# Turned ring of the experts' weights: slots 3 and 4 fetched ahead, one copy of the normed rows, and a token list for the gathers

## The reference

```
def hier_moe(h, rg_w, rg_b, re_w, re_b, w_gate, w_up, w_down):
    gp = softmax(h @ rg_w + rg_b);  g_w, g_idx = top_k(gp, 1)
    el = (h @ re_w + re_b).reshape(N, N_GROUPS, EXPERTS_PER_GROUP)   # 4 groups of 8 experts
    el = el of the chosen group;  ep = softmax(el);  e_w, e_idx = top_k(ep, 2)
    e_w = g_w * e_w / sum(e_w)
    for e in range(32):
        he = silu(h @ w_gate[e]) * (h @ w_up[e])                     # 1024 -> 256
        y = y + comb[:, e:e + 1] * (he @ w_down[e])                  # 256 -> 1024
```

## Time and profile before

| | |
|---|---|
| median of 3 runs | 2420.23 us (2414.74 to 2420.58) |
| the profiled execution | 2420.1 us |
| its span | 2418.2 us |
| mean granted clock of TensorE | 0.989 |
| PE busy | 2305.2 us (95%) |
| DVE, ACT, POOL busy | 979.5, 968.9, 945.1 us |

### The profile page before, as it was taken

One profiled execution on the slowest core, in us unless ns is written; L12 is line 12 of the kernel. 1 busy time (PEld: TensorE's weight loads), 2 busy tenths in 40 slices (PEclk: granted clock), 3 DMA queues, 4 the chain that ended last, 5 costly groups with the idle time before them and its releaser, 6 DMA issues.

```text
span 2418.2 us, 31089 instructions
## 1 busy us (share of the span) xinstructions
PE 2305.2 (95%) x11628; PEld 1872.7 (77%) x11628; DVE 979.5 (41%) x1631; ACT 968.9 (40%) x1611; POOL 945.1 (39%) x757
## 2 busy tenths in 40 slices
PE   7999998888888999999998899999999999999998
PEld 6886786444446998899987778888878887888887
DVE  4377445888884233363335621111321124211113
ACT  3344523666663344343343432222344444322223
POOL 4441241535552433333332145454432222544542
PEclk9999999999999999999999999999999999999999
DMA  5521146999983422312322133333232211233332
GB/s 180 170 76 47 40 156 226 356 391 399 387 322 116 146 84 96 102 53 70 105 86 73 36 92 101 99 93 105 88 106 87 70 53 53 87 105 91 101 98 85
DMA packets 210268, 316.25 MB, mean 131 GB/s; under 512 B 20640, under 2 KB 140192, under 8 KB 200304
## 3 DMA queue, kind: packets, MB, share of 16 engines
q1 hardware_dynamic: 202416, 301.98, 36.5%
q0 software_dynamic: 7744, 12.76, 1.6%
HBM read 300.89 MB, written 22.71 MB: 134 GB/s over the span
## 4 chain that ended last, share of the span: by engine, by line
PE 77%; DVE 6%; issue 5%; DMA 5%; ACT 3%; POOL 2%; SPq 1%; DVEq 0%; ACTq 0%; POOLq 0%
PE bank L873 21%; PE bank L875 21%; PE bank L874 21%; DMA w_ring<-in_w_gate 4%; PE bank L1493 2%; PE bank L1125 2%; POOL w_low L3036 2%; DVE up_low L2553 2%; PE bank L912 1%; PE bank L1104 1%; PE bank L1470 1%; PE bank L1115 1%; PE bank L1480 1%; ACT up_high L1984 1%; PE bank L1297 1%
## 5 line engine op out<-in xcount | busy, mean ns | idle before, releaser
L3036 POOL TENSOR_TENSOR w_low<-raw,w_high 128x512 fp32r<-128x512 f32 x568 | 743.4, 1340 | 1180.7 <-ACT w_high L1730 1148.8
L873 PE MATMUL bank<-h_high,w_high 128*128 128x512 f32 x1088 | 430.8, 396 | 2.3 <-DVE h_low L2297 2.3
L875 PE MATMUL bank<-h_high,w_low 128*128 128x512 f32 x1088 | 425.5, 391 | 0.0
L874 PE MATMUL bank<-h_low,w_high 128*128 128x512 f32 x1088 | 425.1, 391 | 0.0
L1730 ACT ACTIVATE w_high<-raw 128x2048 fp32r<-128x2048 f32 x145 | 276.9, 1909 | 246.8 <-PE bank L875 233.8
L873 PE MATMUL bank<-w_high,h_high 128*128 128x512 f32 (+2 forms) x832 | 328.2, 394 | 13.6 <-ACT qk L2065 4.1
L875 PE MATMUL bank<-w_high,h_low 128*128 128x512 f32 (+2 forms) x832 | 312.3, 375 | 0.0
L874 PE MATMUL bank<-w_low,h_high 128*128 128x512 f32 (+2 forms) x832 | 312.3, 375 | 0.0
L873 PEld LDWEIGHTS bank<-h_high,w_high 128*128 128x128 f32 x1088 | 205.3, 189 | 47.1 <-DVE h_low L2297 6.1
L875 PEld LDWEIGHTS bank<-h_high,w_low 128*128 128x128 f32 x1088 | 205.0, 188 | 43.6
L874 PEld LDWEIGHTS bank<-h_low,w_high 128*128 128x128 f32 x1088 | 205.3, 189 | 40.4
(11 more groups left out here) (378 smaller groups left out, 3371.3 us busy)
## 6 DMA issues: line engine op xcount, KB each, us to landing
raw<-in_ffn_w_gu SPq DMA_DIRECT2D x88, 512.0 KB, 4.5
raw<-in_a_w_in SPq DMA_DIRECT2D x72, 512.0 KB, 4.6
w_ring<-in_w_gate SPq DMA_DIRECT2D x35, 1024.0 KB, 10.1
w_ring<-in_w_up SPq DMA_DIRECT2D x35, 1024.0 KB, 12.3
w_ring<-in_w_down SPq DMA_DIRECT2D x35, 1024.0 KB, 9.2
raw<-in_ffn_w_down SPq DMA_DIRECT2D x40, 512.0 KB, 4.6
raw<-in_w_in SPq DMA_DIRECT2D x34, 512.0 KB, 4.6
raw<-in_b_w_in SPq DMA_DIRECT2D x24, 512.0 KB, 4.6
```

Source lines behind the costliest of these rows:

```text
L873: pe.matmul(out, sta[0], mov[0], start=start, stop=False)
L874: pe.matmul(out, sta[0], mov[1], start=False, stop=False)
L875: return pe.matmul(out, sta[1], mov[0], start=False, stop=stop)
L3036: last = pool.tensor_tensor(out=w_low[:, slot, cols], in0=raw[:, slot, cols], in1=w_high[:, slot, cols].bitcast(F32), op=ALU.subtract)
```

## The change

- The ring is turned: slot 1 goes to `w_ring[0]` and slot 2 to `w_ring[1]`, and `w_ring[0]` now stands where `w_ring[1]` stood. `w_first` is used a second time, for slot 3. So slots 4, 6, ... use `w_ring[0]` and slots 5, 7, ... use `w_ring[1]`.
- Gate and up of slots 3 and 4 are loaded without waiting for `trips`: each as soon as the place it goes to has been split (`m_low` 1 to 4).
- The up half of slot 0 and the gate half of slot 1 are now split by POOL (`up_low_part`, four instructions each), beside the router on DVE. DVE keeps the up half of slot 1.
- The small tables of the router are moved in SBUF, so that `up_low` of buffer 1 is free earlier.
- `d_rows` has one copy of the normed rows (four stores instead of eight). For the gathers, DVE makes a second table, `slot_tokens`, in which 512 is subtracted from the number of a second choice (one more instruction ahead of it, `second`). `slot_rows` still serves the scatters.
- The load of `gw1` (the final norm's gain) goes behind gate and up of slot 6.
- Five semaphores of the router are merged into two. PE's and ACT's first slots are written out up to slot 5, with the ring's place as an argument.

```diff
@@ SP
-        gate(w_ring[1], 1, m_up[1][0])
-        up(w_ring[1], 1, m_up[1][1])
+        gate(w_ring[0], 1, m_up[0][0])
+        up(w_ring[0], 1, m_up[0][1])
...
-            for k in range(2):
-                sp.dma_start(d_rows[k * T + t * P:k * T + (t + 1) * P, :], xn[:, t, :]).then_inc(rows_stored, 16)
+            sp.dma_start(d_rows[t * P:(t + 1) * P, :], xn[:, t, :]).then_inc(rows_stored, 16)
...
         sp.wait_ge(rt_out, NT)
-        down(w_ring[1], 1, m_dn[1])
+        down(w_ring[0], 1, m_dn[0])
+        sp.wait_ge(m_low, 1)
+        gate(w_first, 3, m_gate3)
+        sp.wait_ge(m_low, 2)
+        up(w_first, 3, m_up3)
+        sp.wait_ge(m_low, 3)
+        gate(w_ring[0], 4, m_up[0][0])
+        sp.wait_ge(m_low, 4)
+        up(w_ring[0], 4, m_up[0][1])
...
-        next_up(3, 1)
-        next_up(4, 0)
         sp.wait_ge(m_down, 1)
+        down(w_first, 3, m_dn3)
+        sp.wait_ge(m_low, 5)
+        gate(w_ring[1], 5, m_up[1][0])
+        sp.wait_ge(m_low, 6)
+        up(w_ring[1], 5, m_up[1][1])
+        sp.wait_ge(m_down, 2)
+        down(w_ring[0], 4, m_dn[0])
+        next_up(6, 0)
+        sp.wait_ge(m_low, 8)
         sp.dma_start(gw1[:, :], a["final_norm_g"].partition_broadcast(P)).then_inc(gains_loaded, 16)
-        with sp.Fori(2, n_less) as i:
+        with sp.Fori(3, n_less) as i:
@@ DVE
-        dve.wait_ge(rt_list, 1)
+        dve.wait_ge(rt_counted, 4)
+        step(dve.tensor_scalar(second[:, :], SB[0][0:R, 0:SLOTS], float(T - OOB), float(-T), ALU.is_ge, ALU.mult))
+        dve.scalar_tensor_tensor(out=slot_tokens[:, :], in0=SB[0][0:R, 0:SLOTS], scalar=float(OOB), in1=second[:, :],
+                                 op0=ALU.add, op1=ALU.add).then_inc(rt_slots, 1)
...
-        dve.wait_ge(m_part, 8)
-        up_part(w_first, 0, 1)
+        dve.wait_ge(m_low, 3)
+        up_next(1, 1, 1, w_ring[0])
         rows(0, 0)
         rows(1, 1)
-        up_next(1, 1, 0)
-        up_next(1, 1, 1)
@@ POOL
+        def up_low_part(ring, b, q):
+            for k in range(0, KD, 2):
+                part = (slice(0, P), b, slice(k, k + 2), slice(FE * q, FE * q + FE))
+                last = pool.tensor_tensor(out=up_low[part],
+                                          in0=ring[:, q, FE * k:FE * k + 2 * FE].rearrange("p (k n) -> p k n", k=2),
+                                          in1=up_high[part].bitcast(F32), op=ALU.subtract)
+            last.then_inc(m_low, 1)
+
+        pool.wait_ge(m_part, 8)
+        pool.wait_ge(m_low, 1)
+        up_low_part(w_first, 0, 1)
+        pool.wait_ge(rt_out, NT)
+        pool.wait_ge(m_high, 1)
+        up_low_part(w_ring[0], 1, 0)
         pool.wait_ge(rt_slots, 1)
-        pool.wait_ge(rows_stored, 32 * NT)
+        pool.wait_ge(rows_stored, 16 * NT)
```

More of the change, by code:

```diff
@@ L197, in two_blocks_kernel @@
     x_turn = at("x_turn", 93, [P, KD, T])
[L198 to L211, removed]
+    row_hot = at("row_hot", 29, [P, 2 * NT, R])
+    slot_hot = at("slot_hot", 31, [P, 2 * NT, SLOTS])
+    cut7 = at("cut7", AR + 28.375, [P, 2 * NT, T // R - 1])
+    slote = at("slote", AR + 28.625, [1, SLOTS])
+    cnt = at("cnt", AR + 28.84375, [1, 1])
+    over = at("over", AR + 28.875, [P, 2 * NT])
+    own = at("own", AR + 28.90625, [P, 2 * NT])
+    cut = at("cut", AR + 28.9375, [P, 2 * NT])
+    posf = at("posf", AR + 28.96875, [P, 2 * NT])
+    row_of = at("row_of", AR + 29, [P, 2 * NT])
+    slot_tokens = at("slot_tokens", AR + 96, [R, SLOTS], I32)
+    second = at("second", AR + 28.375, [R, SLOTS])
+    starts = at("starts", AR + 29.03125, [P, NE])
+    more = at("more", AR + 29.1875, [NE, T // R - 1])
+    more_sum = at("more_sum", AR + 29.21875, [NE, 1])
+    more_wide = at("more_wide", AR + 29.25, [NE, P])
     logit = at("logit", AR + 24, [P, NT, 36])
@@ L1298, in up, with down @@
             last.then_inc(m_gu, 1)
-        def down(j, b, uses, come=None):
+        def down(j, ring, loaded, count, come=None):
             pe.wait_ge(m_het, j + 1)
[L1302 to L1307, removed]
+            pe.wait_ge(loaded, count)
+            w = ring[:, 2, :].rearrange("p (k n) -> p k n", k=2)
             pe.wait_ge(m_y, j + 1)
@@ L1325, in _ @@
         up(1, 1, 0)
[L1326 to L1334, removed]
+        down(0, w_first, m_first, 48, lambda: rows_come(1, 2))
+        turn_rows(3, 1)
+        up(2, 0, 1)
+        down(1, w_ring[0], m_dn[0], 16, lambda: rows_come(0, 3))
+        turn_rows(4, 0)
+        up(3, 1, 2)
+        down(2, w_ring[1], m_dn[1], 16, lambda: rows_come(1, 3))
+        turn_rows(5, 1)
+        up(4, 0, 3)
+        down(3, w_first, m_dn3, 16, lambda: rows_come(0, 4))
+        turn_rows(6, 0)
+        up(5, 1, 4)
+        down(4, w_ring[0], m_dn[0], 32, lambda: rows_come(1, 4))
+        with pe.Fori(2, n_less) as i:
+            turn_rows(2 * i + 3, 1)
+            up(2 * i + 2, 0, 2 * i + 1)
+            down(2 * i + 1, w_ring[1], m_dn[1], 16 * i, lambda: rows_come(0, i + 3))
+            turn_rows(2 * i + 4, 0)
+            up(2 * i + 3, 1, 2 * i + 2)
+            down(2 * i + 2, w_ring[0], m_dn[0], 16 * i + 16, lambda: rows_come(1, i + 3))
+        pe.wait_ge(m_he, 2 * n_less + 2)
         pe.matmul(SB[1][0:R, 0:R], ident[:, 0:R], ident[:, 0:R], start=True, stop=True)
         turn_he()
-        down(2 * n_trips - 1, 1, n_trips)
+        down(2 * n_less + 1, w_ring[1], m_dn[1], 16 * n_less)
         phase_mark()
@@ L1985, in up_part, with up_next @@
                            ACT.Copy).then_inc(m_high, 1)
-        def up_next(j, b, uses, q):
-            act.wait_ge(m_up[b][q], 16 * uses)
+        def up_next(j, b, ring, loaded, uses, q):
+            act.wait_ge(loaded[q], 16 * uses)
             if q == 0 and (not isinstance(j, int) or j >= 2):
                 act.wait_ge(m_gu, j - 1)
-            up_part(w_ring[b], b, q)
+            up_part(ring, b, q)
         def rows_high(j, b):
@@ L2014, in _, with period @@
         phase_mark()
+        act.wait_ge(rt_tables, 1)
         rows_high(0, 0)
[L2016 removed]
         n_less = act.value_load(trips[0:1, 1:2], min_val=NE // 2 - 1, max_val=TRIPS - 1)
         n_less2 = act.value_load(trips[0:1, 2:3], min_val=NE // 2 - 2, max_val=TRIPS - 2)
[L2020 removed]
+        def period(j, b, ring, loaded, uses):
             gate(j - 1, 1 - b)
[L2023 removed]
+            up_next(j + 1, 1 - b, ring, loaded, uses, 0)
             rows_high(j + 1, 1 - b)
             turned_he(j - 1)
[L2026 removed]
+            up_next(j + 1, 1 - b, ring, loaded, uses, 1)
         rows_high(1, 1)
[L2029 to L2033, removed]
+        period(1, 1, w_ring[1], m_up[1], 1)
+        period(2, 0, w_first, [m_gate3, m_up3], 1)
+        period(3, 1, w_ring[0], m_up[0], 2)
+        with act.Fori(2, n_less) as i:
+            period(2 * i, 0, w_ring[1], m_up[1], i)
+            period(2 * i + 1, 1, w_ring[0], m_up[0], i + 1)
+        period(2 * n_less2 + 2, 0, w_ring[1], m_up[1], n_less2 + 1)
         gate(2 * n_less2 + 2, 0)
```

79 lines of the change are left out of this document (41 added, 38 removed).

## The result

| | before | after |
|---|---|---|
| median of 8 runs | 2419.0 us (2414.74 to 2420.58) | 2425.1 us (2420.66 to 2426.87) |
| ratio, 95% interval | | 1.0021 (1.0012 to 1.003) |
| profiled execution | 2420.1 us | 2421.2 us |
| DVE, ACT, POOL busy | 979.5, 968.9, 945.1 us | 981.7, 968.9, 956.2 us |
| HBM written | 22.71 MB | 20.61 MB |

The forecast was 2424 us, "within 0.3%", on the slow side. The medians differ by 6.1 us; the ratio puts the cost at 5.1 us, or 0.21% (its interval: 2.9 to 7.3 us).

A forecast was written before the change was run, and what follows sets the result against it. PE bounds the kernel (busy 95%), except in the expert loop, which waits about 24 us for DMA. A 7.2 us delay less 3.4 bought back by loads ahead gives 2420.1 + 3.8 = 2423.9 us; range 2413 to 2430.

The forecast's parts named there:

- The hold: In the router, POOL's eight instructions hold eight DVE instructions, so `el` and everything behind it are 7.3 us late.
- The first rival: The router on DVE is hardly held by POOL: 4 us less than before, 2416 us; chance 0.13.
- What is late next: Behind the router, PE, row table and gathers are 7.3 us late; the experts start 7.2 us later.
- That moves along: After `keep_clock`, PE's start on the first rows, at 415.92 after 1.00 us of issue, shifts with the 7.3 us delay.
- The third rival: PE stays at 1.2 GHz into the first slots: slower beyond 0.3%, at most 2432 us; chance 0.16.
- What the loads ahead buy: In the expert loop, earlier loads of slots 3 and 4 buy back 3.4 of 7.2 us, leaving 3.8.
- the ring's: Slot 6 reuses slot 4's place; its up matrix lands 4.9 us after issue, 1.2 us later than before.
- The term for `gw1`: Loading `gw1` behind slot 6's up matrix costs 2.0 us, making the loads 3.2 us late.
- From there the queue is full in both, with the same bytes to move: From slot 5's down matrix on, DMA is full in both kernels, so the loop ends 3.2 to 4.5 us late.
- The sign given for this: ACT's first wait for a gate matrix in the loop comes two to four slots later than slot 7's.
- The second rival: Idle DMA ahead of the loop is really filled: 2410 us if half of it, 2396 if all; chance 0.11.
- it goes through to the end: Behind the loop nothing changes and PE is the bound, so the 3.8 us reach the end: 2423.9 us.

The follow-up runs named there:

- e1: The changed kernel with POOL splitting nothing and DVE doing those splits behind the router: 2416.41 us against 2419.25 for the kernel before, ratio 0.9995.
- e2: The kernel before plus eight POOL TENSOR_TENSOR of 128x512 beside the router, results unused: 2424.18 us against 2419.25, ratio 1.0023.
- e3: The changed kernel with POOL splitting only slot 0's up half, DVE both halves of slot 1: 2419.89 us, ratio 1.001 to the kernel before.
- e9: The kernel before plus POOL copies of 128x512 beside the router, results unused: 2420.24 us in one execution, against 2420.68 for one run of before.
- e4: The kernel before with only the one copy of normed rows and the token table for the gathers: 2418.34 us, ratio 0.9998.
- e6: The changed kernel with the `gw1` load moved behind the loop's last down matrix: 2424.57 us, ratio 1.0022 to the kernel before.
- e5: The changed kernel without POOL splits, `gw1` load moved behind the loop's last down matrix: 2417.07 us against 2418.84 for the kernel before, ratio 0.9996.
- e8: The kernel before with only the `gw1` load moved behind the loop's last down matrix: 2417.07 us, ratio 0.9993.
- e7: The changed kernel with POOL splitting in sixteen instructions of 256 elements instead of eight of 512: 2424.82 us in one execution.

## Why the prediction was right

**The hold: right, in kind and size.** Eight windows of POOL and eight held instructions were counted; the eight take 8.59 us instead of 1.56, so 7.03, against 7.3 forecast. The difference is POOL's own time: 9.9 us from first to last, where 2 x 5.04 and a gap between were counted. The first rival (no hold) is out by e1 and e2, and e3 shows about half the price for half the work. The Trainium skill (GPSIMD Engine Reference, Key points) names the held kind rightly; that the holder may be a plain copy, and that the hold lasts to the end of its instruction, are shown here by e9's 0.58 and after's 1.27.

**What is late next: right in e2, 1 us less in after.** With the hold alone everything moves by 7.2 as forecast. The pause has a small price of its own, which the prediction left out. PE comes out of 8.64 us of idling at 1.2 GHz (0.50 from 403 to 411; 0.37 us for a matmul that takes 0.26 in e1), and DVE waits 0.44 us for its counts, which it hadn't; so `slot_rows` is 7.6 us late, against e4. In after, part of it is given back: `keep_clock` runs at full clock again (3.70 us against e4's 5.40) and PE starts on the first rows 25.24 us behind `goh` against e4's 19.32, which is 5.9 late. "That moves along" was wrong by about 1.3 us: this cover has slack once its clock is up, and then the gather is what PE waits for. The third rival (the clock stays low into the first slots) didn't happen: the clock is 1.00 from 422 on in after. In e6 it is 0.91 from 422 to 440, and its Silu of slot 1 is no later for it (42.22 against 42.53).

**What the loads ahead buy: right in sum.** The forecast was 7.2 late at the start of the loop and 3.8 at its end. Measured against e4 and e8 it is 5.9 to 6.1 at the Silu of slot 1 and 4.0 to 4.6 at the last. So 1.4 to 2.1 us are gained along the loop, not 3.4, and not all of it by the loads ahead, since the loop of e2 is 1.1 shorter than that of before without them. What they buy is the 1.1 to 1.7 us between slots 1 and 6, where the turned ring has no wait left: 39.1 us for 5 slots is the 7.82 each of slots 2 to 5. The step that was mis-sized is the ring's: I put slot 6's up matrix 1.2 late instead of 7.2, a gain of 6.0, and took 2.0 off for `gw1`. Even with no hold (e1), the gain at the last Silu is 2.4, where that way of counting gives 4. One part of it can be read in e1: the up matrix was to land in 4.9 us, as into an idle queue, but slot 6's gate matrix was still on its way, and it took 6.5. The term for `gw1`, 2.0, measures 0 to 0.7 (e5, e6, e8).

Both go back to the sentence "From there the queue is full in both, with the same bytes to move". DMA share 1.01 from 463.6 on is as foretold, but a lead in landed weights decays before that (4.6, 2.7 and then 1.5 us in e1), while DMA waits for places (shares of 0.60 and 0.83), and half a megabyte more or less in the full stretch doesn't show at its price of 1.3 us. The sign given for this, a first wait two to four slots later, failed: it was one slot. Why a byte in the loop costs less than its time at 397 GB/s isn't settled. The second rival (idle DMA filled) is out. From `goh` + 8 to `goh` + 70, e1, whose experts start when those of before do, has a DMA share of 0.66 against 0.69; after has 0.57 and e2, which has the hold without the loads ahead, 0.55.

**The sum is near partly by luck.** The delay at the start of the loop was put 1.1 to 1.3 us too high and what comes back along the loop 1.3 to 2.0 too high. The two errors cancel, and 3.8 stands against 4.0 to 4.6.

**Behind the loop.** The prediction had "it goes through to the end", so 3.8 in all; the medians differ by 6.1. Between the last Silu and the end the profiled executions take 1698.8 us (before), 1698.1 (e1), 1699.0 (e2), 1698.7 (e4), 1698.1 (e5), 1698.5 (e8) and 1699.5 (e9), but 1700.6 (after), 1702.5 (e6), 1700.3 (e3) and 1702.8 (e7), with the same instructions. The four longest are those in which POOL splits for the turned ring. Held side by side, DVE's instructions keep the same distance within 0.1 us almost all the way. The differences arise in the first 140 us, again in the 60 us that begin 555 us behind the last Silu, and in e6 once more, shortly after. Stretches of these 60 us in before, e4 and after (granted clock in the third column from the end):

```profile
1276.32:1336.32 60.00, 51.38 (x331) 42.06 (x331) 33.82 (x65) 24.21 (x60) 14.97 (x12) 0.94 0.22 65
```

```profile
1271.54:1331.54 60.00, 51.54 (x317) 42.16 (x317) 32.68 (x63) 24.20 (x60) 14.97 (x12) 0.89 0.23 66
```

```profile
1275.56:1335.56 60.00, 51.62 (x308) 42.33 (x307) 31.76 (x61) 23.14 (x58) 14.97 (x12) 0.89 0.20 56
```

Where the clock is 0.94 here (before, e1, e5, e8), nothing is lost against before; where it is 0.89 (e4, e9, after, e3) or 0.86 (e2, e6, e7), 2.9 to 3.6 us are. So PE is at 1.2 GHz here for longer in some executions than in others, and that happens with the old ring and without a hold too (e4). What after loses behind the loop, 1.8 us, is 3.2 here less 1.4 ahead of it. All four kernels with the split have the lower clock here, but so have three of the other seven, and with one profile each it isn't shown whether the split makes it more likely. So of the 6.1 us, 4.0 to 4.6 are shown to arise up to the end of the loop; the rest is of the size of what this clock gives and takes, and the ratio's 5.1 leaves little of it.

None of the versions beats the kernel before by what can be measured: e1, e5 and e8 lie at 0.9993 to 0.9996 with 1 inside their intervals. All three are faster than the changed kernel, whose interval begins at 1.0012.

## What to carry to other kernels

An engine without work isn't free to take some: before work goes to POOL, look at what DVE does in that time, and if it is a chain of small instructions with two SBUF inputs, the chain grows by a good part of POOL's busy time (here 7.0 of 9.9 us, 3.9 of 4.95, 6.6 of 11.2 in small pieces, and 1.9 of 4.57 with copies). Loads issued earlier are worth no more than the waits up to the place where the ring's depth holds them back: some 4 MB ahead bought 1.1 to 1.7 us here. After the filled hole look for the one that opens behind it, and price the lead where it ends, not where it begins. A busy share of 1.0 in the DMA engines says that they are never idle, not that every byte taken away is time gained: half a megabyte less gave 0 to 0.7 us. And where two traces differ by a few microseconds, line them up at one instruction and see where they part, before a place is given the blame.

## What the runs showed of the hardware

- A DVE instruction of 128x16 with two SBUF inputs took 1.27 us beside a 1.24 us TENSOR_TENSOR of POOL, 0.72 beside one of 0.70 and 0.58 beside a copy of 0.57; a reduction kept its 0.17 beside all of them.
- Eight fp32 matmuls of 512 columns took 5.66 (before), 5.40 (e4), 5.24 (e2), 4.79 (e8) or 3.70 us (after, e9) in the same place, by where the low clock lay. With 3.70, PE was through before the gathered rows had come.
- POOL subtracts 4 x 128x512 in 4.95 us (after) and copies 8 x 128x512 in 4.57 us (e9).
- The same instructions behind the loop took 1698.1 to 1702.8 us. In one stretch of 60 us, a mean granted clock of 0.86 to 0.89 instead of 0.94 cost 2.9 to 3.6 us.
